# Down projections of a two-block model: low parts of half the plain weight slots made by accumulating DMAs, and 13 seven-product slots per pass in place of 11

## What is computed

```python
f = jnp.square(jax.nn.relu(h @ w_ff1[l])) @ w_ff2[l]        # first block
h = h + jnp.square(jax.nn.relu(m)) @ w_down[l]              # second block (m = norm(h) @ w_up)
```

## Time and profile before

| | |
|---|---|
| median of 3 runs | 2220.45 us (2220.36 to 2221.12) |
| profiled execution, first to last instruction | 2219.3 us |
| PE, DVE, ACT, POOL busy | 99%, 73%, 52%, 4% |
| granted clock of TensorE, mean | 0.999 |
| read from HBM | 398.90 MB |

### The profile page before, as it was taken

One profiled execution on the slowest core, in us unless ns is written; L12 is line 12 of the kernel. 1 busy time (PEld: TensorE's weight loads), 2 busy tenths in 40 slices (PEclk: granted clock), 3 DMA queues, 4 the chain that ended last, 5 costly groups with the idle time before them and its releaser, 6 DMA issues.

```text
span 2219.3 us, 32872 instructions
## 1 busy us (share of the span) xinstructions
PE 2195.5 (99%) x13128; PEld 1892.6 (85%) x13128; DVE 1613.8 (73%) x2013; ACT 1163.2 (52%) x1682; POOL 93.2 (4%) x66
## 2 busy tenths in 40 slices
PE   8999999999999999999999999999999999999998
PEld 7888988888888888888898988888888888888886
DVE  7878565665454599899886578847454547998997
ACT  6433465543443466566664466646434345665665
POOL 0553000000000000000000000000000000000000
PEclk9999999999999999999999999999999999999999
DMA  8364445555556666667654533455565565666663
GB/s 328 121 153 161 151 134 211 168 190 189 189 188 188 187 194 207 195 205 258 199 166 144 172 115 98 136 196 163 187 189 189 189 189 173 215 201 195 209 202 114
DMA packets 169923, 402.65 MB, mean 181 GB/s; under 512 B 15296, under 2 KB 30912, under 8 KB 165968
## 3 DMA queue, kind: packets, MB, share of 16 engines
q1 hardware_dynamic: 158496, 394.83, 55.3%
q10 hardware_dynamic: 11312, 6.22, 1.2%
HBM read 398.90 MB, written 2.13 MB: 181 GB/s over the span
## 4 chain that ended last, share of the span: by engine, by line
PE 94%; DVE 4%; ACT 1%; issue 1%; DMA 0%; SPq 0%; DVEq 0%; ACTq 0%
PE ps L768 21%; PE ps L773 11%; PE ps L841 7%; PE ps L842 6%; PE ps L843 6%; PE ps L657 5%; PE ps L857 3%; PE ps L856 3%; PE ps L858 3%; PE ps L665 3%; PE ps L666 3%; PE ps L667 3%; PE ps L1075 2%; PE ps L1077 2%; PE ps L1076 2%; PE ps L679 2%
## 5 line engine op out<-in xcount | busy, mean ns | idle before, releaser
L2497 DVE TENSOR_TENSOR w_low<-raw_weights,w_high 128x1024 fp32r<-128x1024 f32 (+1 forms) x403 | 474.3, 1215 | 422.1 <-ACT w_high L1574 418.3
L1574 ACT ACTIVATE w_high<-raw_weights 128x1024 fp32r<-128x1024 f32 (+1 forms) x378 | 377.4, 1046 | 408.0 <-PE ps L773 279.8
L768 PE MATMUL ps<-x_split,w_high 128*128 128x512 f32 x2048 | 494.1, 391 | 1.7 <-DVE x_split L2485 1.7
L768 PEld LDWEIGHTS ps<-x_split,w_high 128*128 128x128 f32 x2048 | 374.6, 188 | 74.2 <-issue 3.0
L773 PEld LDWEIGHTS ps<-x_split,w_low 128*128 128x128 f32 x2048 | 265.8, 191 | 12.1
L773 PE MATMUL ps<-x_split,w_low 128*128 128x256 f32 x2048 | 269.4, 283 | 0.0
L841 PE MATMUL ps<-w_high,x_split 128*128 128x512 f32 x672 | 262.0, 390 | 0.5 <-issue 0.4
L842 PE MATMUL ps<-w_low,x_split 128*128 128x512 f32 x672 | 261.5, 389 | 0.0
L843 PE MATMUL ps<-w_high,x_split 128*128 128x512 f32 x672 | 261.4, 389 | 0.0
L2582 DVE TENSOR_TENSOR w_low<-raw_weights,w_high 128x1024 fp32r<-128x1024 f32 x168 | 197.8, 1219 | 1.7 <-ACT w_high L1689 1.6
L1689 ACT ACTIVATE w_high<-raw_weights 128x1024 fp32r<-128x1024 f32 x168 | 167.6, 1045 | 0.0
(11 more groups left out here) (376 smaller groups left out, 3657.9 us busy)
## 6 DMA issues: line engine op xcount, KB each, us to landing
raw_weights<-in_w_ff SPq DMA_DIRECT2D x128, 1024.0 KB, 5.4
raw_weights<-in_w_up SPq DMA_DIRECT2D x64, 1024.0 KB, 5.2
raw_weights<-in_w_down SPq DMA_DIRECT2D x64, 1024.0 KB, 5.5
raw_weights<-in_w_in SPq DMA_DIRECT2D x62, 1024.0 KB, 5.3
raw_weights<-in_w_out SPq DMA_DIRECT2D x32, 1024.0 KB, 4.9
raw_weights<-in_w_mem_kv SPq DMA_DIRECT2D x7, 1024.0 KB, 14.6
residual<-in_xT SPq DMA_DIRECT2D x2, 2048.0 KB, 13.9
region<-t_table ACTq DMA_DIRECT2D x1, 3072.0 KB, 18.9
```

Of the source, the lines that this page charges most:

```text
L768: nc.tensor.matmul(hidden_ps(g)[:, c], w[:, P * c:P * c + P], xs[:, kt], start=(kt == 0), stop=False, skip_group_check=True)
L1574: nc.scalar.activation(split_slot(wh_t, k)[:, r], ring_slot(n)[:, r], ACT.Copy).then_inc(rounded, 1)
L2497: V.tensor_tensor(split_slot(wl_t, k)[:, r], ring_slot(n)[:, r], split_slot(wh_t, k)[:, r].bitcast(f32), ALU.subtract).then_inc(split_read ...
```

## The change

In every pass the summed slots are now 2, 4, 6 ... 26 (`SUMMED`, 13) and the odd slots 3, 5 ... 27 between them are plain (`ADDED`, 13). Slots 0, 1, 28, 29, 30 and 31 stay plain as they were. In an odd slot DVE subtracts nothing from the weights. ACT rounds each half of the slot and then writes the negated rounding of the same half into `wl_t` (`negated`). POOL waits for each half and issues a DMA of 128 x 1024 floats that reads the same weights from HBM once more and adds them onto the half (`lows_added`). PE waits for both DMAs of the slot (`low0_added` and `low1_added` by turns). DVE keeps `split_ready` counting by a small memset, after both halves are negated.

```diff
@@ -456,7 +456,8 @@
-        SUMMED = (2, 5, 7, 10, 12, 15, 17, 20, 22, 25, 27)
+        SUMMED = tuple(range(2, 28, 2))
+        ADDED = tuple(range(3, 28, 2))
@@ -830,6 +836,9 @@
                     if banks[0] == 0:
                         pe.wait_ge(chunk_ready, PLAIN0[name] + n + 1)
                         pe.wait_ge(split_ready, 2 * (k + 1))
+                        if r in ADDED:
+                            a = added_count(name, h, r)
+                            pe.wait_ge(low_added[a % 2], 32 * (a // 2 + 1))
@@ -1687,6 +1696,8 @@
                 for half_ in range(2):
                     w = slice(SLOT // 2 * half_, SLOT // 2 * (half_ + 1))
                     nc.scalar.activation(split_slot(wh_t, k)[:, w], ring_slot(n)[:, w], ACT.Copy).then_inc(rounded, 1)
+                    if r in ADDED:
+                        nc.scalar.activation(split_slot(wl_t, k)[:, w], ring_slot(n)[:, w], ACT.Copy, scale=-1.0).then_inc(negated, 1)
@@ -2240,9 +2251,21 @@
+            def lows_added(name, w):
+
+                for h in range(2):
+                    for r in ADDED:
+                        k, a = SPLIT0[name] + plain_count(h, r), added_count(name, h, r)
+                        for q in range(2):
+                            pool.wait_ge(negated, 2 * a + q + 1)
+                            pool.dma_start(split_slot(wl_t, k)[:, HALF * q:HALF * q + HALF],
+                                           w[2 * P * r + P * q:2 * P * r + P * q + P, 1024 * h:1024 * h + 1024].bitcast(mybir.dt.float32r),
+                                           accum_op=ALU.add).then_inc(low_added[a % 2], 16)
+
@@ -2576,6 +2600,12 @@
                     dve.wait_ge(chunk_rounded, PLAIN0[name] + c + 1)
                     V.tensor_tensor(x_low, pair_of(r), x_high.bitcast(f32), ALU.subtract).then_inc(chunk_ready, 1)
+                    if r in ADDED:
+                        dve.wait_ge(rounded, 2 * (SPLIT0[name] + PAIRS * h + r) + 2)
+                        dve.wait_ge(negated, 2 * added_count(name, h, r) + 2)
+                        dve.wait_ge(split_ready, 2 * (SPLIT0[name] + PAIRS * h + r))
+                        V.memset(st[:, 38:39], 0.0).then_inc(split_ready, 2)
+                        return
```

More of the change, by code:

```diff
@@ L471, in summed_count, with added_count @@
             return len(SUMMED) * h + sum(q < r for q in SUMMED)
+        def added_count(name, h, r):
+            return len(ADDED) * (2 * (name == "ff2_2") + h) + sum(q < r for q in ADDED)
         def slot_before(count, slots):
@@ L627, in program @@
         bank_done, quad_used = sem("bank_done"), sem("quad_used")
+        negated, low_added = sem("negated"), [sem(f"low{i}_added") for i in range(2)]
         HIDDEN0 = {"ff1_1": 0, "ff1_2": FT // 4}
@@ L2245, in _ @@
             gather("outn", 0, near_sq, 0)
+            lows_added("ff2_1", A["w_ff2"])
             pool.wait_ge(act_done, at("mlan", "sq", 0))
@@ L2252, in _ @@
             gather("window", 1, xo, 8)
+            lows_added("ff2_2", A["w_down_2"])
         @block.vector
```

## The result

The changed kernel takes 2525.28 us (median of 4 runs, 2524.05 to 2527.68), the kernel before 2220.41: a ratio of 1.1371, 95% interval 1.1355 to 1.1387. I had said slower, and why, but 2306 us with a range up to 2390. The profiled execution of after has a span of 2522.3 us, 303.0 more than before.

A forecast was written before the change was run, and what follows sets the result against it. PE was taken to bound the kernel; 91.3 us of waits for the adding DMAs less 5.4 us for dropped matmuls made +85.9 us on 2219.3, and with 1.15 us to the runs' median 2306 us, range 2232 to 2390.

The forecast's parts named there:

- What bounds the kernel: Down projections: PE, busy 99% of the span and hardly waiting, so time is the number of matmuls times 0.2268 us.
- 5.4 us for the matmuls: PE in the four down passes: 24 matmuls fewer at 0.2268 us each save 5.4 us, all on the path.
- DVE needs the relief: DVE in two alternating slots: 8.8 us of work in 10.21, but 11.2 if it kept two subtractions of 1.22.
- ACT's added copies: ACT in odd slots: two negated copies, 0.955 us each in a row, raise two slots' work from 6.8 to 8.75 us.
- The budget of 3.24 us: Odd slots: time for the second adding DMA between ACT's last negated copy at 901.76 and PE's arrival at 905.00.
- 28 links: Four down passes: seven links of a slot chain each, every link adding the DMA's time beyond 3.24 us.
- D = 6.5 us: Second adding DMA, POOL's wake-up to semaphore: a 1 MB load's 6.1 us in company plus 0.4, giving 91.3 us of waits.
- the 9.9 that I called the upper bound: Adding DMA's time from above: 512 KB took 9.9 us in the crowd at the start; that end gave +181 us.
- The 3.5 us for a plain 512 KB: Adding DMA's time from below: a straight line through SP's landings of 576 KB and 1024 KB; that end gave +1.9 us.
- The rival of the DMA engines as the bound: Down stages: added bytes counted twice need 13.1 us per two slots, 2.86 over 10.21: +143, 2363 us; chance 0.12.
- The clock: TensorE in the down stages: waits lower its clock for one fifth of them, 130 us more, some 2440 us; chance 0.03.
- the 1 to 4.5 us: Sign expected in the profile after: PE waits this long on a DMA into `w_low` in 13 slots of a pass.

The follow-up runs named there:

- e11: Changed kernel, odd slots from 5: DVE subtracts one half, one adding DMA makes the other; negated copies made ahead, PE's `w_low` matmuls last: 2223.09 us.
- e10: Changed kernel with 12 seven-product slots per pass, no adding DMAs, DVE subtracting in every plain slot, PE's `w_low` matmuls last: 2224.17 us.
- e12: Changed kernel with adding DMAs only in slots 5, 9 ... 25, DVE subtracting elsewhere, negated copies made ahead, PE's `w_low` matmuls last: 2234.49 us.
- e1: Changed kernel's slot alternation without adding DMAs or negated copies; DVE subtracts for every plain slot: 2265.62 us.
- e4: Changed kernel, but in odd slots PE does the 16 matmuls without `w_low` first and waits for the DMAs only before the other 8: 2414.16 us.
- e2: Kernel before plus twelve groups of extra 512 KB GpSimd DMAs, adding or plain, single or paired, into a buffer nobody reads: 2221.21 us.
- e3: Changed kernel with plain copying DMAs in place of the adding ones, same queue, bytes and waits, leaving out the sum: 2369.34 us.
- e8: Changed kernel with both negated copies made ahead of the preceding seven-product slot, in ACT's idle time; adding DMAs begin at slot 5: 2309.11 us.
- e13: e8 with DVE's memset placed ahead of the next sums, so the ring's load of the slot four later starts earlier: 2289.35 us.
- e7: Changed kernel without DMAs or negated copies: in odd slots GpSimd subtracts the first half of the weights, DVE the second: 2313.57 us.

## Why the prediction was wrong, point by point

- **What bounds the kernel; 5.4 us for the matmuls.** The bound was right, and the 24 matmuls are gone (13104 for 13128). That they are worth 5.4 us is not shown by the changed kernel, since the term cancels in its balance of 303 us; e11, e10 and e12 fit it to 0.7 to 1.6 us by the count above.
- **DVE needs the relief.** Right, by e1: the overload that the prediction worked out, about 1 us in each of 52 pairs, is the price of the alternation without the DMAs, 50 us (35.1 in waits, 14.3 in a longer busy time).
- **ACT's added copies, 0.955 us each, and its order.** Right. In the earlier trace rows time they end at 897.85 + 3.91; after, from 894.52 to 898.40, 3.88 us. One reading was off by a matmul and changes nothing: 892.76 in the earlier trace rows is the start of the thirteenth, the twelfth starts at 892.53.
- **The budget of 3.24 us and 28 links.** Right. There are 28 long waits of PE, and e4, which widens the budget alone by 3.63 us, takes 110 us of them for 101.6 expected. What I had not seen is that a single chain carries them, since the wait of one lets the other's DMA land.
- **D = 6.5 us: the step that failed.** PE's waits ask for a D of 8.7 + 3.24 = 11.9 us, beyond the 9.5 of the range and the 9.9 that I called the upper bound; 28 x 8.7 is the 243 us measured. I took the row of a 1 MB load beside another queue (6.1 us) and added 0.4. But an adding DMA costs 2.9 us of all engines for 512 KB, nearly twice what a load of as many bytes costs; the second lands behind its partner (6.1 us for a single one and 7.8 for a pair in e2); and the held-up ring sends its loads at the same moment. e3 shows that the adding is worth 3.9 of the 10.3 us; how the rest splits between partner and loads no run shows. A pair and one load are 6.1 + 3.1 = 9.2 us of engine time alone, before any latency. The 3.5 us for a plain 512 KB, my lower end, were too low too: two single loads of SP of just that size landed in 5.7 and 6.1 us in the trace of before, rows that I passed over, and the plain DMAs of e3 took 6.4. I had both numbers' makings: the doubling stood in the text as a rule, and as the rival of throughput, but not in the term.
- **The rival of the DMA engines as the bound.** Wrong for the changed kernel, where the waits leave the engines idle between bursts (0.69 over 889 to 1009), right as soon as the waits are gone: 13.1 us for two slots was its number, 12.15 are e8's, and 2363 us its time against 2309.
- **The clock.** I gave it 0.03 and left it out of the sum. PE's busy time is 64 us too long here. At the 0.29 us that a wait costs at full clock in e1, 29 waits make 8 of them; the other 56 or so, an estimate, are the clock's, about 2 us for each long wait. The waits came as single pieces of 9 us and not as the 1 to 4.5 us that I had spread over all odd slots, and PE's mean busy share, from which I argued, said nothing about them: e3, with PE at 95%, loses 56 us in the same way.

Together: the waits are 152 us over (243.5 for 91.3) and PE's busy time 64, which makes 216 of the 217 us between the forecast's span and the measured one.

The two rows of the trace of before that the lower end of D passed over:

```profile
raw_weights<-in_w_mem_kv SPq DMA_DIRECT2D x1, 512.0 KB, 6.1
raw_weights<-in_w_ukv SPq DMA_DIRECT2D x1, 512.0 KB, 5.7
```

## What to carry to other kernels

Before work is moved to a DMA, write down how long after its last input the consumer needs it, and put the landing of the slowest DMA of that kind in the worst company against it; an adding DMA cost nearly twice a load per byte here, and its partner and the loads that a stall sets free are part of the company. When a full matrix engine gets waits of several microseconds, charge the slow restart behind each as well as the wait, here some 2 us. Making the input earlier (e8) was worth 216 us, adding less (e11) 86 more, and still only the old time was left, since PE had been full from the start.

## What the runs showed of the hardware

- 512 KB through GpSimd's queue: 1.3 us of all 16 engines as a copy, 2.7 to 2.9 us when added to the destination (e2, beside the ring's loads); 0.53 (e3) and 0.86 us (after) of GpSimd for the issue.
- TensorE's granted clock read 1.00 up to 896 us, in a wait from 891.6 to 901.4, then 0.50 to about 906.6. In e3 it read 0.50 in the first 4 us of work behind a wait of 3.5 us. In e8 it read 0.65 from 917.4 to 920 us, behind a wait of 2.0 us. PE's busy time grew by 56 to 64 us with 29 to 33 waits, whether they took 3.1 us each (e3) or 8.7 (after), and by 14 us with 50 waits of 0.7 us at full clock (e1).
- Two loads of 1 MB and two adding DMAs of 512 KB kept the engines at a share of 0.98 for 12.15 us in e8 and for 11.7 us in e13.
- A DVE instruction of 0.69 us took 2.79 us beside a GpSimd subtraction of 2.8 us (e7).
